# The last output tile of a streaming encoder trunk, formed in column parts of 384 and 128 in place of 256 and 256

## What is computed

```python
def rmsnorm(x, g):
    y = x * rsqrt(mean(x * x, axis=-1, keepdims=True) + 1e-6)
    return y * g

for layer in range(2):
    h = h + mixer(rmsnorm(h, norm_mix_g[layer]))
    gate, val = split(rmsnorm(h, norm_ffn_g[layer]) @ w_up[layer])     # 2 x 2816 features
    h = h + (silu(causal_dwconv(gate)) * val) @ w_down[layer]          # 2816 -> 1024
return rmsnorm(h, norm_final_g)
```

## Time and profile before

| | |
|---|---|
| Median of 3 runs | 1081.69 us (1081.07 to 1082.23) |
| Profiled execution | 1083.43 us |
| its span, first to last instruction | 1081.6 us |
| TensorE busy | 1068.1 us (99%) |
| VectorE busy | 639.7 us (59%) |
| ScalarE busy | 463.8 us (43%) |
| GpSimd busy | 188.1 us (17%) |

### The profile page before, as it was taken

One profiled execution on the slowest core, in us unless ns is written; L12 is line 12 of the kernel. 1 busy time (PEld: TensorE's weight loads), 2 busy tenths in 40 slices (PEclk: granted clock), 3 DMA queues, 4 the chain that ended last, 5 costly groups with the idle time before them and its releaser, 6 DMA issues.

```text
span 1081.6 us, 15533 instructions
## 1 busy us (share of the span) xinstructions
PE 1068.1 (99%) x5556; PEld 865.7 (80%) x5556; DVE 639.7 (59%) x874; ACT 463.8 (43%) x732; POOL 188.1 (17%) x243
## 2 busy tenths in 40 slices
PE   9999999999999999999999999999999999999997
PEld 7887578888888888888888777888888888888886
DVE  6799754566666666633334775656666666643332
ACT  6455565444434343422233565553444344422221
POOL 8999720400000000000000222310000000000000
PEclk9999999999999999999999999999999999999998
DMA  6551024232222222222324111223222222222322
GB/s 228 166 126 41 20 84 175 78 117 98 97 97 97 97 97 97 97 98 99 108 94 156 60 51 50 98 97 99 96 97 97 97 97 97 97 98 97 117 78 78
DMA packets 36459, 107.27 MB, mean 99 GB/s; under 512 B 7808, under 2 KB 10112, under 8 KB 36160
## 3 DMA queue, kind: packets, MB, share of 16 engines
q1 hardware_dynamic: 36416, 106.69, 29.7%
HBM read 102.09 MB, written 3.15 MB: 97 GB/s over the span
## 4 chain that ended last, share of the span: by engine, by line
PE 88%; DVE 2%; issue 1%; POOL 0%; ACT 0%; DVEq 0%
PE bank L1569 28%; PE bank L1570 27%; PE bank L1571 27%; PE bank L1593 1%; PE bank L1957 1%; PE bank L1934 1%; PE bank L1779 1%; PE bank L1714 1%; DVE wlo L1037 1%; PE bank L1707 0%; PE bank L1742 0%; PE bank L1736 0%; POOL pbuf L670 0%; DVE outb L1540 0%; DVE wbuf L1226 0%
## 5 line engine op out<-in xcount | busy, mean ns | idle before, releaser
L1569 PE MATMUL bank<-xhi,whi 128*128 128x512 f32 x960 | 376.5, 392 | 0.1
L1570 PE MATMUL bank<-xlo,whi 128*128 128x512 f32 x960 | 373.8, 389 | 0.0
L1571 PE MATMUL bank<-xhi,wlo 128*128 128x512 f32 x960 | 373.7, 389 | 0.0
L1037 DVE TENSOR_TENSOR wlo<-raw,whi 128x1024 fp32r<-128x1024 f32 x177 | 233.4, 1320 | 209.2 <-ACT whi L687 208.7
L687 ACT ACTIVATE whi<-raw 128x1024 fp32r<-128x1024 f32 x177 | 187.0, 1057 | 327.2 <-PE bank L1571 304.8
L1569 PEld LDWEIGHTS bank<-xhi,whi 128*128 128x128 f32 x960 | 180.3, 188 | 39.4 <-issue 0.8
L1571 PEld LDWEIGHTS bank<-xhi,wlo 128*128 128x128 f32 x960 | 180.3, 188 | 37.9
L1570 PEld LDWEIGHTS bank<-xlo,whi 128*128 128x128 f32 x960 | 180.4, 188 | 37.2 <-issue 0.3
L1569 PE MATMUL bank<-ahi,whi 128*128 128x512 f32 (+1 forms) x374 | 142.4, 381 | 0.0
L1570 PE MATMUL bank<-alo,whi 128*128 128x512 f32 (+1 forms) x374 | 142.2, 380 | 0.0
L1571 PE MATMUL bank<-ahi,wlo 128*128 128x512 f32 (+1 forms) x374 | 142.2, 380 | 0.0
(11 more groups left out here) (258 smaller groups left out, 1057.4 us busy)
## 6 DMA issues: line engine op xcount, KB each, us to landing
raw<-wstream SPq DMA_DIRECT2D x177, 512.0 KB, 3.2
xin<-xT SPq DMA_DIRECT2D x8, 256.0 KB, 5.4
raw<-wstream SPq DMA_DIRECT2D x8, 256.0 KB, 5.0
h<-xT SPq DMA_DIRECT2D x1, 2048.0 KB, 8.5
u_scratch<-uperm SPq DMA_DIRECT2D x1, 1024.0 KB, 5.5
uc<-u_scratch SPq DMA_DIRECT2D x8, 128.0 KB, 4.9
bandsb<-band SPq DMA_DIRECT2D x1, 1024.0 KB, 4.8
outT<-outb SPq DMA_DIRECT2D x2, 512.0 KB, 2.9
```

The costliest lines, as they stand in the source:

```text
L1037: V.tensor_tensor(wlo[:, t % RING, :], raw[:, t % RAWS, :], whi[:, t % RING, :].bitcast(f32), ALU.subtract).then_inc(lo_done, 1)
L1569: MM(dst, wh, rhi, start=start, stop=False)
L1570: MM(dst, wh, rlo, start=False, stop=False)
L1571: return MM(dst, wl, rhi, start=False, stop=stop)
```

## The change

The two column parts become 384 and 128 columns (`HALF`). Everything that is indexed by `HALF` follows: the matmuls of the last tile, additions, squares, means, factors, scalings and transfers. On VectorE, the whole first part is scaled before the second part is added. The second part is scaled in three instructions (tile 7, tiles 4 to 6, tiles 0 to 3) in place of five, and sent in two transfers of four tiles in place of four of two tiles. The transfers of the first part have 768 KB each, those of the second part 256 KB each.

```diff
-    HALF = [slice(0, SEQ // 2), slice(SEQ // 2, SEQ)]
+    HALF = [slice(0, 3 * P), slice(3 * P, SEQ)]
...
-        for hf, m0, m1, need in ((0, 0, 4, 1), (0, 4, 8, 3), (1, 6, 8, 5), (1, 4, 6, 6), (1, 2, 4, 7),
-                                 (1, 0, 2, 8)):
+        for hf, m0, m1, need in ((0, 0, 4, 1), (0, 4, 8, 3), (1, 4, 8, 5), (1, 0, 4, 6)):
             sp.wait_ge(out_done, need)
             sp.dma_start(outT[:, m0:m1, HALF[hf]], outb[:, m0:m1, HALF[hf]]).then_inc(out_saved, 16)
-        sp.wait_ge(out_saved, 16 * 6)
+        sp.wait_ge(out_saved, 16 * 4)
...
-            V.tensor_tensor(out, out, rstd[:, HALF[hf]].unsqueeze(1).to_broadcast([P, m1 - m0, SEQ // 2]),
+            V.tensor_tensor(out, out, rstd[:, HALF[hf]].unsqueeze(1).to_broadcast([P, m1 - m0, HALF[hf].stop - HALF[hf].start]),
                             ALU.mult).then_inc(out_done, 1)
...
         scale_half(0, 0, 4)
+        scale_half(0, 4, KB - 1)
+        scale_last(0)
         add_half(1)
-        scale_half(0, 4, KB - 1)
         dve.wait_ge(half_added, 2)
-        scale_last(0)
         dve.wait_ge(half_factor, 2)
         scale_last(1)
-        scale_half(1, KB - 2, KB - 1)
-        for m in (4, 2, 0):
-            scale_half(1, m, m + 2)
+        scale_half(1, 4, KB - 1)
+        scale_half(1, 0, 4)
```

## The result

| | before | after |
|---|---|---|
| Median | 1081.59 us | 1084.19 us |
| Ratio, with its 95% interval | | 1.0024 (1.0015 to 1.0032) |
| Profiled execution | 1083.43 us | 1084.39 us |
| its span | 1081.6 us | 1082.6 us |
| First product of the last tile | 1057.08 | 1055.56 |

The change costs 2.6 us, or 0.24%. One of the 13 runs of the changed kernel took 3792 us and is left out of the ratio. The two spans differ by only 1.0 us, because the stretch ahead of the last tile was 1.52 us shorter in this execution. The two executions are therefore compared from the first product of the last tile: 27.04 - 24.52 = 2.52 us (the ends of the spans are known to 0.1 us), which is what the medians show.

The account below looks back on a forecast made before the run. TensorE was taken to bound the kernel until its last products, then a short serial tail. 3.91 + 0.43 + 0 - 0.66 - 0.86 = +2.8 us gave a forecast of 1084.5 us, range 1082.3 to 1086.5.

Parts of the forecast that it names:

- 66 products of 384 columns: First part of the last tile on TensorE: products 0.170 to 0.175 us apart, 0.1725 taken, +3.91 us.
- Mean of the first part: Four plain f32 passes on TensorE's own path, 1.29 us over 384 columns, +0.43 us.
- 66 products of 128 columns: Second part on TensorE: weight loads of 0.825 ns per column keep the step at 0.1135 us, 0 us gained; chance 0.71.
- Start of the last addition: TensorE delivers the second part +4.34 us later, at 1077.47 us.
- Addition to first transfer: Serial tail on 128 columns, from the last addition to the last part's first transfer: -0.66 us.
- First transfer to end of span: Two last 256 KB transfers in 512-byte pieces, 34 ns a piece, 1.09 us each: -0.86 us.
- VectorE's order: First part scaled before the last addition: VectorE free at 1077.45, 0.02 us before TensorE delivers, so no cost, no slack.
- the line through 1 and 4 KB: Estimate for output transfers from the larger two piece sizes: 27 ns per 512-byte piece.
- The line through the 256-byte gathers: Estimate for output transfers from the smaller two piece sizes: 41 ns per 512-byte piece.
- Plain f32's pace: Rival, second part: narrow products step at 0.213 us, 6.6 us more, 1091.1 us; chance 0.17.
- The fast step: Rival, second part: products step near 0.057 us, VectorE's new order then holds the addition, 1083.1 us; chance 0.09.

## Why the prediction was right, point by point

The direction, the mechanism and the place were as forecast; 1084.5 was predicted and 1084.19 measured. The terms from the first product of the last tile on:

| Term | forecast | measured |
|---|---|---|
| 66 products of 384 columns | +3.91 (3.74 to 4.07) | +4.18 (66 x 0.1768 against 7.49) |
| Mean of the first part | +0.43 | +0.50 (0.70 + 0.66 against 0.86) |
| 66 products of 128 columns | 0 (-0.4 to +1.1) | -0.10 (66 x 0.112) |
| Start of the last addition | +4.34 | +4.50 (20.55 against 16.05) |
| Addition to first transfer | -0.66 | -0.60 (2.87 against 3.47) |
| First transfer to end of span | -0.86 (-1.52 to -0.45) | -1.38 (3.62 against 5.00) |
| Sum | +2.8 | +2.52 |

The first three rows are steps times 66 and record times, and come to +4.58. The start of the addition is read from the trace itself: +4.42 with the old order, where TensorE alone sets it, and 0.08 more behind VectorE.

- **The first part** was 0.27 us dearer than summed and left its bounds: 384 columns cost 0.1768, more than three quarters of 512. The step isn't a line through the widths, as I took it to be, and it isn't fixed by the width either: with the buffers moved by 64 bytes it was 0.1737, inside the bounds.
- **The second part** is where the change fails, and the step from the load of 0.825 ns a column held: 0.112 for 128 columns and 0.11 for 64, 0.060 with half of the weights. For 256 columns the load isn't the whole of it: with the buffers moved by 64 bytes they step at 0.120, while 128 columns stay at 0.111. One of my arguments for it was weak, though. The load row busy for 4.00 of 4.00 us shows nothing by itself, because one record lasts 0.187 us and is busy beside the next at any step under that; at 384 columns, where no load binds, the row reads the same:

```profile
1060.00:1064.00 4.00, 4.00 (x24) 4.00 (x23) 0.00 (x0) 0.00 (x0) 0.00 (x0) 1.00 0.00 0
```

- **VectorE's order** was forecast to be ready 0.02 us before TensorE, and was 0.08 late. The tie was real: the chain after goes through VectorE, and the old order moves the addition by only that much. What I hadn't priced is what the order protects. With the old one, the first part's second transfer blocks the last two, 1.37 us longer from the addition to the end. Even with the new one that transfer's last piece landed at 1079.80 and the next transfer's first piece moved at 1079.88, where I had 0.6 us between them.
- **The transfers** were mis-sized by 0.52 us. 512-byte pieces moved at 278 to 302 GB/s in the half microseconds from 1080 to 1081.5, where I had 240, against 345 for 1 KB. One of them takes 27 ns (the median in the trace), which is just what the line through 1 and 4 KB gave; by it the term would have been 2 x 0.86 + 1.96 - 5.0 = -1.31. The line through the 256-byte gathers misled: it took their 110 GB/s as 37 ns a piece, and in the trace one of them takes 44 ns (the median), longer than an output piece of twice its size. (The end of that line, 41 ns, gives -0.42 and not the -0.45 I wrote.) The Trainium skill, "DMA: Bandwidth & Descriptors", section Specifications, would have the full rate at 512 bytes, which was -1.52; the row shows 302 and not 345, and the term came out at -1.38, much nearer to that than to mine.
- The number was in part luck. The first part came out 0.27 us dearer and the transfers 0.52 cheaper than forecast, and these errors cancel in part, so the sum was closer than its worst term.
- **The rivals.** Plain f32's pace was excluded by the row of 0.112. The fast step didn't come by itself; made by halving the weights it gave 1082.82 where 1083.1 was worked out. "TensorE: Matmul & The Clock Gate" of the Trainium skill, section Back-to-back issue gap, has 81 ns for 128 columns; here it was 112, with float32r operands.

## What to carry to other kernels

A product that loads its own weights has a floor, here 0.11 us for 128 float32r weight columns, and splitting columns below it buys nothing: price a split by the load and not by the columns, and split evenly when both parts stand at that floor. When work is put ahead of a late addition, compare its end with the arrival of the operand, and look at which transfer goes out when, since at the end of a kernel the queue can be worth more than the engine. A row that is busy all the time isn't a bound where its records overlap.

## What the runs showed of the hardware that was not expected

The step of a matmul depends on where its moving operand's rows begin. For `ahi` and `alo` with 512 columns it was 0.2333, 0.2267 and 0.229 us at the old place and 64 and 128 bytes on; with 256 columns 0.1133, 0.120 and 0.118, so the place that is slow for the wide product is fast for the narrow one. Over 990 products the 64 bytes gave 5.6 us, twice what the change cost. The same place is not good for all, though: `ohi` and `olo`, the attention's operands, moved too and went from 0.229 to 0.232 and 0.233.

The record has one more operand, `xchi` and `xclo` of the first mixer, whose rows begin at the same place as those of `ahi`. The trace of the kernel before:

```profile
74.78 0.39 PE L1571 MATMUL bank<-xchi,wlo 128*128 128x512 f32 x1
...
77.58 0.39 PE L1571 MATMUL bank<-xchi,wlo 128*128 128x512 f32 x1
```

12 steps take 2.80 us, 0.2333 each, and after the two moves they are 0.2267 and 0.229 to 0.230: in another stage, the same values at the same places as `ahi`. By the kernel's layout the rows of `ohi` begin 896 bytes on from those of `ahi` (within 2 KB). Counted within 256 bytes from where `xhi` begins, all twelve readings at 512 columns (four pairs of operands, at three places of the buffers) then fall on four values: 0.2267 at 0, 0.229 to 0.230 at 64, 0.232 at 128, 0.233 at 192. That is a fit to runs that were made for something else; no run was made to test it. What in the memory causes it, and why the halves in `down` alone stepped at 0.1178, is not settled.
